# Streaming encoder step: attention's depth chosen by tile, the sample's third stream of keys loaded first, and the selection's rounds placed anew

## The reference

```python
score = einsum('bqhl,bqh->bql', relu(s), w)          # 8 indexer heads
score = where(adm, score, -inf)
_, idx = lax.top_k(score, topk)                      # 256 keys of a prompt query, 132 of a sample query
logits = einsum('bqhgd,bqjhd->bqhgj', q, k_sel) * HD ** -0.5
p = softmax(where(valid, logits, -inf))
o = einsum('bqhgj,bqjhd->bqhgd', p, v_sel)           # 16 heads, 4 key/value heads of 64
```

## Time and profile before

| | us |
|---|---|
| median of 3 runs (2817.14 to 2819.47) | 2818.42 |
| the profiled execution | 2823.1 |
| its span | 2821.2 |
| in it the attention phase, 321 to 640 | 319 |
| PE busy in the attention phase | 299.06 |
| DVE busy there | 243.64 |
| ACT busy there | 240.81 |

### The profile page before, as it was taken

How to read it: one execution, slowest core, us unless ns; L and a number is a source line. 1 busy time by engine, 2 the same in 40 slices (tenths; PEclk the granted TensorE clock), 3 DMA queues, 4 the chain that set the end, 5 groups by cost and what they waited for, 6 DMA issues and landing times. The chain is left out here.

```text
span 2821.2 us, 43795 instructions
## 1 busy us (share of the span) xinstructions
PE 2734.0 (97%) x16007; PEld 2405.3 (85%) x16007; DVE 2010.4 (71%) x3073; ACT 1302.6 (46%) x2140; POOL 368.2 (13%) x389
## 2 busy tenths in 40 slices
PE   8899999999999999999999999999999999999998
PEld 8889877667889988999888988877888999889987
DVE  4389789843597789877975166637269877887787
ACT  3277668882344444544442144434133544445433
POOL 2222011110000000000012155447000000000000
PEclk9999999999999999999999999999999999999999
DMA  4422531234132322223214333347312323222231
GB/s 151 115 55 92 142 81 24 46 90 157 58 121 78 105 81 75 92 81 110 70 54 147 102 111 115 124 138 278 112 67 91 102 73 109 71 85 80 92 103 74
DMA packets 202173, 279.04 MB, mean 99 GB/s; under 512 B 29282, under 2 KB 138786, under 8 KB 202035
## 3 DMA queue, kind: packets, MB, share of 16 engines
q1 hardware_dynamic: 201890, 276.68, 30.7%
q10 hardware_dynamic: 144, 0.52, 0.1%
HBM read 220.13 MB, written 57.03 MB: 98 GB/s over the span
## 5 line engine op out<-in xcount | busy, mean ns | idle before, releaser
L1671 DVE TENSOR_TENSOR h<-mlp_dn_acc,h 128x512 f32<-128x512 f32 x308 | 200.9, 684 | 19.9 <-PE mlp_dn_acc L1522 19.1
L1522 PE MATMUL mlp_dn_acc<-end_w_hi,early 128*128 128x512 f32 x400 | 157.8, 395 | 0.0
L1522 PE MATMUL mlp_dn_acc<-end_w_hi 128*128 128x512 f32 x392 | 155.1, 396 | 2.7 <-DVE end_w_lo L1644 1.4
L1522 PE MATMUL mlp_dn_acc<-end_w_lo,end_w_hi 128*128 128x512 f32 x392 | 155.0, 395 | 0.0
L660 PE MATMUL acc<-mid_w_hi,mid_xT_hi 128*128 128x512 f32 x320 | 130.7, 409 | 2.7 <-DVE mid_xT_lo L246 2.1
L660 PE MATMUL acc<-mid_w_lo,mid_xT_hi 128*128 128x512 f32 x320 | 125.5, 392 | 0.0
L660 PE MATMUL acc<-mid_w_hi,mid_xT_lo 128*128 128x512 f32 x320 | 125.4, 392 | 0.0
L2962 ACT ACTIVATE att_logits<-att_logits,att_neg_max 128x528 f32<-128x528 f32 (+8 forms) x144 | 111.3, 773 | 23.6 <-DVE att_neg_max L3025 23.1
L2934 ACT ACTIVATE att_probs_T<-att_psT 128x512 f32<-128x512 f32 (+3 forms) x224 | 98.6, 479 | 39.7 <-PE att_psT L2835 36.9
L1522 PE MATMUL mlp_dn_acc<-mid_w_hi 128*128 128x512 f32 x294 | 114.4, 389 | 0.0
L1522 PE MATMUL mlp_dn_acc<-mid_w_hi,mid_w_lo 128*128 128x512 f32 x294 | 114.4, 389 | 0.0
(11 more groups left out here) (595 smaller groups left out, 9197.2 us busy)
## 6 DMA issues: line engine op xcount, KB each, us to landing
mlp_pool_w<-x_sums SPq DMA_DIRECT2D x84, 576.0 KB, 3.7
mlp_pool_w<-in_ffn_w_up SPq DMA_DIRECT2D x42, 512.0 KB, 4.7
spare_w<-in_ffn_w_down SPq DMA_DIRECT2D x32, 512.0 KB, 3.8
proj_w_raw<-in_a_w_in SPq DMA_DIRECT2D x8, 1024.0 KB, 6.0
mid_w_raw<-in_ffn_w_down SPq DMA_DIRECT2D x16, 512.0 KB, 4.3
end_w_raw<-in_ffn_w_down SPq DMA_DIRECT2D x16, 512.0 KB, 4.0
x_sums<-mlp_pool_w SPq DMA_DIRECT2D x24, 288.0 KB, 2.1
spare_w<-in_b_w_in SPq DMA_DIRECT2D x6, 1024.0 KB, 7.0
```

The lines of the kernel that those rows point to most:

```text
L1522: mm = pe.matmul(dst, lhs(c, f), rhs(a, f), start=(n == 0 and not onto), stop=(n == 2 * len(TERMS) - 1), skip_group_check=onto)
L1671: dve.tensor_tensor(dst, acc, dst, ALU.add).then_inc(added, 1)
```

## The change

1. Planner of the projection: an empty entry is put in after the first of `steps`, so that each later step of the sample's indexer comes one projection unit later.
2. Depth: `lag(n)` is 3 for heads of the sample and of tiles 3, 0 and 2 (`DEEP`) and stays 2 for the others. `turn` and `turn_out` of head n come in iteration n + lag(n), and the four quad tables move by the same lag. In the sample `stream_values` comes one iteration later and ahead of `turn`, and `finish` of its groups one iteration later.
3. In tile 3 the copies of odd heads out of the transposes' bank go from ACT to DVE. From tile 3 on each copy waits for the one before it, whichever engine makes it.
4. Loads: keys of stream 2 are issued first; the prompt's keys are loaded in two halves, the second of them after the keys of stream 3. POOL waits for the half that it needs.
5. Rounds: 15 in the sample (`SAMPLE_ROUNDS`, up to two in a head), and in tiles 7, 6, 5, 4 and 1 in the heads named by `ROUND_HEADS`.

```diff
-        steps = [[("s_new", 0, 0), ("s_turn", 0, 0)]]
+        steps = [[("s_new", 0, 0), ("s_turn", 0, 0)], []]
...
-    VALUES_AT = {quad_at(q) + 6 + 2 * half: (q, half) for q in range(NQ) for half in range(2)}
-    OUT_AT, BACK_AT, FINISH_AT = ({quad_at(q) + later: q for q in range(NQ)} for later in (9, 10, 11))
+    DEEP = (SAMPLE, 3, 0, 2)
+    lag = lambda n: 3 if tile_at(n) in DEEP else 2
+    TURN_AT = {}
+    for n in range(N):
+        TURN_AT.setdefault(n + lag(n), []).append(n)
+    VALUES_AT = {quad_at(q) + lag(quad_at(q)) + 4 + 2 * half: (q, half) for q in range(NQ) for half in range(2)}
+    OUT_AT, BACK_AT, FINISH_AT = ({quad_at(q) + lag(quad_at(q)) + later: q for q in range(NQ)} for later in (7, 8, 9))
+    on_dve = lambda n: tile_at(n) == 3 and n % 2 == 1
...
+    SAMPLE_ROUNDS = {3: 1, 5: 1, 6: 2, 8: 2, 9: 1, 11: 1, 12: 2, 13: 2, 14: 2, 15: 1}
+    ROUND_HEADS = {7: (0, 1, 2, 3), 6: (0, 1, 2), 5: (0, 1, 2), 4: (0, 1, 2, 3), 1: (0, 2)}
...
-        now = [left.pop(0)] if left and n >= 3 and n not in PARTS else []
+        room = SAMPLE_ROUNDS.get(n, 0) if n < HEADS else n not in PARTS and n % GH4 in ROUND_HEADS.get(tile_at(n), ())
+        now = [left.pop(0) for _ in range(min(room, len(left)))]
...
+                load_keys(2)
                 load_values(0)
                 sp.dma_start(nv[:, :, :], v_new.rearrange("(b t) c -> t b c", t=DEC_T)).then_inc(new_v_in, 16)
-                sp.dma_start(kin[:, :, :, :].rearrange("p t v d -> p t (v d)"), k_out.rearrange("(t p) c -> p t c", p=P))\
-                    .then_inc(k_loaded, 16)
-                load_keys(2)
+                load_prompt_keys(slice(0, NT_P // 2))
                 load_values(1)
                 load_keys(3)
+                load_prompt_keys(slice(NT_P // 2, NT_P))
...
-                    if 2 <= n < N + 2:
-                        turn(n - 2)
-                    if 3 <= n < HEADS + 3:
-                        stream_values(n - 3)
+                    if 4 <= n < HEADS + 4:
+                        stream_values(n - 4)
+                    for m in TURN_AT.get(n, ()):
+                        turn(m)
...
+                def turn_out(n):
+                    for x, i in enumerate(bank_of[n]):
+                        dve.wait_ge(turned_out, i)
+                        dve.wait_ge(turned, i + 1)
+                        dve.wait_ge(values_done, (n - HEADS) // GH4 - 1)
+                        out, turned_bank = turned_parts(n, x, i)
+                        dve.tensor_copy(out, turned_bank).then_inc(turned_out, 1)
...
-                    if GH4 <= n < HEADS + GH4 and n % GH4 == GH4 - 1:
-                        finish(n // GH4 - 1)
+                    for m in TURN_AT.get(n, ()):
+                        if on_dve(m):
+                            turn_out(m)
+                    if GH4 < n <= HEADS + GH4 and n % GH4 == 0:
+                        finish(n // GH4 - 2)
```

More of the change, by code:

```diff
@@ L2585, in attention_phase @@
     key_bank, prep_bank, bank_of, banks = {}, {}, {}, 1
-    for n in range(-1, N + 2):
+    for n in range(-1, N + 3):
         if n + 1 < N and tile_at(n + 1) == SAMPLE:
@@ L2592, in attention_phase @@
             banks += 1
-        if n >= 2:
-            nb = -(-length(n - 2) // (4 * P))
-            bank_of[n - 2] = list(range(banks, banks + nb))
+        for m in TURN_AT.get(n, ()):
+            nb = -(-length(m) // (4 * P))
+            bank_of[m] = list(range(banks, banks + nb))
             banks += nb
@@ L2667, in attention_phase, with turned_parts @@
         o_stored = [last_stored, b.sem("o_stored1")]
+        def turned_parts(n, x, i):
+            c0, c1 = 4 * x * P, min(4 * (x + 1) * P, length(n))
+            rows = P if (c1 - c0) % P == 0 else c1 - c0
+            cols = max(c1 - c0, P)
+            return probs_T[0:rows, probs_slot(n), c0:c0 + cols], psT[0:rows, i % 2, 0:cols]
         with b.program() as block:
@@ L2922, in turn_out @@
                     for x, i in enumerate(bank_of[n]):
+                        if n > DVE_FROM:
+                            act.wait_ge(turned_out, i)
                         act.wait_ge(turned, i + 1)
@@ L2930, in turn_out @@
                             act.wait_ge(values_done, (n - HEADS) // GH4 - 1)
[L2931 to L2935 removed]
+                        out, turned_bank = turned_parts(n, x, i)
+                        act.activation(out, turned_bank, ACT.Copy).then_inc(turned_out, 1)
                 def oT_copy(q):
@@ L2941, in oT_copy @@
                     act.activation(oT[:, q % 2, :], pv[:, q % 2, 0:2 * P], ACT.Copy).then_inc(oT_out, 1)
-                for n in range(-1, N + 6):
+                for n in range(-1, N + 7):
                     if n + 1 in key_bank:
@@ L2951, in _ @@
                         q_hi(1)
-                    if 2 <= n < N + 2:
-                        turn_out(n - 2)
+                    for m in TURN_AT.get(n, ()):
+                        if not on_dve(m):
+                            turn_out(m)
                     if n in OUT_AT:
@@ L3005, in _ @@
                                     q_new[HD:P, pair, :, :].rearrange("p g (b t) -> p g b t", t=DEC_T)).then_inc(qs_done, 1)
-                for n in range(N + 8):
+                for n in range(N + 9):
                     if n < N:
```

16 lines of the change are left out of this document (9 added, 7 removed).

## The result

The changed kernel took 2826.53 us (median of 13 runs, 2824.32 to 2829.28), the kernel before 2819.47 (13 runs on the same chip, 2814.88 to 2822.09). The ratio is 1.0024, with a 95% interval of 1.0017 to 1.0032: slower, by about 7 us, where 9 us less were forecast. It lies outside the range. The profiled execution took 2825.04 us with a span of 2823.3.

The account below looks back on a forecast made before the run. PE, busy 97% of the span, bounds the kernel; its 20 us idle in attention and low clock bound the gain. Terms 5.5 - 0.4 + 0.7 + 0 - 0.2 + 1.3 + 1.3 + 0.6 = 8.8 us less: 2809.6, range 2806 to 2813.

Parts of the forecast that it names:

- The sample and tile 7: Attention's first two stretches, up to tile 6: 5.5 us less, between 3.5 and 7, with short iterations kept.
- A: PE's 3.22 us wait for stream 2's keys in the sample: 1.4 us left, gain 1.6 to 3.3.
- B: PE's 1.92 us wait in the sample's head 8 for DVE's `k_lo`: gone, with its low spell.
- DVE is behind PE, and it sets the pace: End of the sample: DVE ends head 15 at 383.9 us, PE starts tile 7 at 381.2.
- Tile 1: Forecast together with tile 4, where DVE's rounds cost 2.5 us more: 0 for both, between -2 and +1.
- C: PE's 3.08 us wait at tile 3's start for ACT's exponential behind `q_hi`: stays with its low spell, -0.2.
- Tile 3's copies: DVE's copies in tile 3: 0.7 us each, between 0.5 and 1.2, hidden under PE's work, 0 gain.
- D: PE's 1.39 us wait at tile 0's start for ACT's exponential: down to 0.3; low spell most likely gone, 1.3 more.
- The projection: PE's waits ahead of attention, 2.98 and 1.88 us, become 2.6 and 2.7: 0, within 1.5.
- The waits only move: Rival, 0.14: busy DVE holds PE up in tile 7 or at tile 1; 5 us lost, 2815.
- Low clock stays: Rival, 0.15: remaining and new waits in the sample and tile 0 still lower the clock; 5 us less, 2813.4.
- Copies in turn: Rival, 0.07: in tile 3 and the handover at tile 0, ACT's and DVE's copies delay each other; about 2825.

Follow-up runs that it names:

- three edits: The changed kernel with the sample's values product back behind the turn, tile 1's round two heads later and no empty projection step: 2820.68 us, ratio 1.0002.

## Why the prediction was wrong, point by point

- **The sample and tile 7, +3.8 us where -5.5 was forecast: the step that failed.** "Without waits an iteration of PE takes 4.25 us in a `PREP` head and 3.70 else. The change moves no matmul away, so these hold." They became 4.98 and 4.55. `stream_values` ahead of `turn` was counted only for the cover it gives DVE's `k_lo`; that it was itself the cover of ACT's copy, the next user of the bank, was not asked. The prediction took both, short iterations and the cover for `k_lo`. The runs show that one excludes the other: 4.98 us with the cover, or 4.25 with waits for `k_lo` of 0.88 and 1.76. That the order alone makes the iterations long, and that undoing it makes them short, is shown from both sides; what it costs in all is 5.3 us between two kernels that begin alike.
- **Where the 9.3 us between forecast and profile lie.** Up to iteration 4 it is 13.4 us from the attention's start where 11.4 were forecast; from there to tile 7 55.6 where 48.6 were (eleven iterations of 0.73 or 0.85 more make 8.5; 0.6 of them fall ahead of iteration 4, and 0.7 was forecast as a wait for `k_lo(9)`); tile 7 takes 50.1 where it had 48.8. That is 10.3, and 0.9 had been held back for the clock. The order is the largest part and not all of it: with order and rounds both mended, 112.6 us is still 2.8 above the forecast's 109.8.
- **A** is 1.70 us, where 1.4 was worked out, but not for the reason given. The landing was mis-sized: POOL's first copy starts 9.67 us after the attention's first matmul, where the row of `kin` gave 8.53, and in all twelve profiles where PE waits for the block it gets it 10.3 to 10.7 us after it, where 9.1 were forecast. The wait is short here because the low spell at the start makes PE late; where the start is at the full clock, with three edits, it is 2.53 with a low spell behind it. (By ring order alone, as the Trainium skill's "DMA: Bandwidth & Descriptors", "Queues, rings and completion order" was weighed there, nothing would have been left of A.) The trace went the other way, past the row. **B** went, as said; the wait of 0.7 for `k_lo(9)` did not come, because the longer iterations gave DVE the time.
- **"DVE is behind PE, and it sets the pace"** did not come to pass for the same reason. With the short iterations it did: `k_lo` waits of 0.88 and 1.76 us.
- **Tile 6** gained 1.1 where a loss of 0.4 was forecast, tile 5 0.66 (0.7), tile 4 0.7. PE was busy for all 41.54 us of tile 6: its own work was less than the 42.6 it was held to need.
- **Tile 1** lost 2.3. Together with tile 4 that is 1.6 lost, inside the forecast's 2 lost to 1 gained, but by luck: the range was for DVE's added rounds, and those cost nothing that shows. The round in tile 1 was priced by the row of a round, 1.13 us, without its last step and without a look at what POOL does at that time. No row of before showed the two side by side.
- **C** +0.3 (0.2). **Tile 3's copies** 0.69 us each, hidden, as said. **D** 0.53 (0.3), tile 0's clock 1.00. But the gain of D and tile 0 is 2.56 us only against an execution with a low spell there; against the kernel before profiled again, whose wait is the same 1.40 us with the clock at 1.00, it is 1.0. The low spell was counted as the wait's due; it came in two of six profiles with that wait.
- **The projection** +1.7 in the mean where 0 within 1.5 was said: the term was too small. 1.2 of it is left between profiles with the same low spells.
- **The rivals.** "The waits only move" had the right stretch and the wrong engine: ACT's copy, not DVE, took the gain back. "Low clock stays" came true in part and elsewhere: not behind A in the first profile of the changed kernel, but at the attention's start. "Copies in turn" did not happen; its price of about 2825 is 15 us above the forecast of 2809.6, not 8, and that it lies near the measured time is luck.

## What to carry to other kernels

Before you move a piece of work on an in-order queue, list what runs on the other engines during it: the piece is cover for someone, and taking it from one wait gives it to another. Here a product of 1.4 us covered a bank's copy in every iteration, and was moved to cover a wait that came once. When a second change makes that wait worse (two rounds ahead of a head that needs DVE), look at their place too: with the short iterations it was worth 3.5 us (68.65 to 65.19 in the sample), where putting the order back gave 1.4 in the profile and 2.8 by the ratios. Compare profiles that begin alike: the same work took 62.42 us in one and 65.19 in another. And when work is moved to another time, look at what GpSimd does then, not only at the queue of the engine it moves on.

## What the runs showed of the hardware that was not expected

- A VectorE `TENSOR_SCALAR` of 128x384 within SBUF took 0.36 us with GpSimd idle, and 4.62 us when it started 0.12 us behind a GpSimd `TENSOR_TENSOR` of 4.53 us on SBUF.
- The same wait in the same place is followed by a low clock in one execution and not in another: 1.39 us at tile 0's start, then a mean clock of 0.90 over the tile and 17.07 us; and 1.40 us, 1.00 and 15.53 us. Of six executions with this wait two had the low clock.
- The same work in the sample took 62.42 us in one execution and 65.19 in another: PE waited 1.51 us for the doubled block with the clock at 1.00 behind it, or 2.59 us with 0.50 from 333.3 to 340.0.
- The part of the program behind attention, with the same instructions in all kernels, took 2170.2 to 2171.4 us in the four executions without a stretch at the lower clock at its start, and 2173.6 to 2176.1 in the fourteen with one.
